# The layout of a routing matrix between SBUF and DRAM, and the place of two reads in one DMA queue

## The reference, cut to what matters

```python
def block(xb):                                   # 128 tokens
    q = (xb @ w_q).reshape(PEER_BLOCK, PEER_HEADS, 2, PEER_DHALF)
    s = jnp.einsum('thpd,hpkd->thpk', q, subkeys)
    s1, i1 = lax.top_k(s[:, :, 0], PEER_TOPK)    # 8 heads, 2 x 128 subkeys, the best 16 of each
    s2, i2 = lax.top_k(s[:, :, 1], PEER_TOPK)
    ...                                          # best 16 of the 256 pair sums: idx, softmax g
    act = gelu(einsum('td,thkd->thk', xb, u[idx]))
    return einsum('thk,thkd->td', g * act, v[idx])
```

## Time and profile before

| | |
|---|---|
| device time, 3 runs | 4415.58, 4419.44 (median), 4424.55 us |
| span of the profiled execution | 4411.2 us |
| PE busy | 4020.6 us (91%) |
| DVE busy | 3174.1 us (72%) |
| ACT busy | 2085.5 us (47%) |
| first layer's experts, down slots | about 1107 to 1686 us of the span |
| second layer's experts, down slots | about 2380 to 2765 us |

### The profile page before, as it was taken

One profiled execution on the slowest core, in us unless ns is written; L12 is line 12 of the kernel. 1 busy time (PEld: TensorE's weight loads), 2 busy tenths in 40 slices (PEclk: granted clock), 3 DMA queues, 4 the chain that ended last, 5 costly groups with the idle time before them and its releaser, 6 DMA issues. The chain is left out here.

```text
span 4411.2 us, 68760 instructions
## 1 busy us (share of the span) xinstructions
PE 4020.6 (91%) x24324; PEld 3590.5 (81%) x24324; DVE 3174.1 (72%) x7302; ACT 2085.5 (47%) x4105; POOL 557.2 (13%) x433
## 2 busy tenths in 40 slices
PE   8979999999999998889999999699887999988898
PEld 5669999999777776689998777598876989887687
DVE  7778999997777776679866677564676656548665
ACT  4434433775333333345675555344455444435453
POOL 0000034223222220005770000000000000000000
PEclk9989999999999999999999999899998999999899
DMA  6245588889999993768898888344435444434353
GB/s 240 96 143 185 177 310 296 287 303 355 332 319 314 325 317 138 232 191 214 221 242 260 262 253 255 131 185 129 139 102 178 185 157 185 157 119 126 131 195 133
DMA packets 417963, 939.83 MB, mean 213 GB/s; under 512 B 53258, under 2 KB 242938, under 8 KB 402058
## 3 DMA queue, kind: packets, MB, share of 16 engines
q1 hardware_dynamic: 362380, 801.86, 54.7%
q0 software_dynamic: 55296, 134.31, 9.8%
HBM read 842.60 MB, written 93.42 MB: 212 GB/s over the span
## 5 line engine op out<-in xcount | busy, mean ns | idle before, releaser
L173 DVE TENSOR_TENSOR w_low__2<-w_raw__2,w_high__2 128x512 fp32r<-128x512 f32 x544 | 361.8, 687 | 123.2 <-ACT w_high__2 L168 111.6
L161 PE MATMUL hidden<-hT_high__2,w_high 128*128 128x384 f32 (+1 forms) x1280 | 423.8, 331 | 11.7 <-DVE w_low L173 11.1
L168 ACT ACTIVATE w_high<-w_raw 128x512 fp32r<-128x512 f32 x576 | 341.5, 625 | 180.7 <-PE side L163 80.4
L173 DVE TENSOR_TENSOR w_low<-w_raw,w_high 128x512 fp32r<-128x512 f32 x576 | 381.3, 685 | 62.3 <-ACT w_high L168 62.2
L162 PE MATMUL hidden<-hT_low__2,w_high 128*128 128x384 f32 (+1 forms) x1280 | 419.4, 328 | 0.0
L163 PE MATMUL hidden<-hT_high__2,w_low 128*128 128x384 f32 (+1 forms) x1280 | 419.2, 328 | 0.0
L168 ACT ACTIVATE w_high__2<-w_raw__2 128x512 fp32r<-128x512 f32 x544 | 321.8, 623 | 85.0 <-DMA w_raw__2<-in_peer_v 30.7
L161 PE MATMUL hidden__3<-hT_high__4,w_high__2 128*128 128x256 f32 x1152 | 326.9, 284 | 0.1
L163 PE MATMUL hidden__3<-hT_high__4,w_low__2 128*128 128x256 f32 x1152 | 323.3, 281 | 0.0
L162 PE MATMUL hidden__3<-hT_low__4,w_high__2 128*128 128x256 f32 x1152 | 323.2, 281 | 0.0
L161 PEld LDWEIGHTS hidden<-hT_high__2,w_high 128*128 128x128 f32 x1280 | 242.8, 190 | 13.5 <-issue 9.4
(11 more groups left out here) (975 smaller groups left out, 12142.2 us busy)
## 6 DMA issues: line engine op xcount, KB each, us to landing
w_raw<-in_peer_u SPq DMA_DIRECT2D x128, 512.0 KB, 5.5
w_raw<-in_peer_v SPq DMA_DIRECT2D x128, 512.0 KB, 5.4
w_raw__2<-in_peer_u SPq DMA_DIRECT2D x128, 512.0 KB, 4.3
w_raw__2<-in_peer_v SPq DMA_DIRECT2D x128, 512.0 KB, 5.0
activated_dram<-activated SPq DMA_DIRECT2D x128, 192.0 KB, 6.4
routing_dram<-routing SPq DMA_DIRECT2D x24, 1024.0 KB, 9.6
routing_chunk<-routing_dram SPq DMA_DIRECT2D x16, 1536.0 KB, 13.9
activated_again<-activated_dram SPq DMA_DIRECT2D x128, 192.0 KB, 5.6
```

The source lines that it names most:

```text
L161: nc.tensor.matmul(out, lhs[0], rhs[0], start=start, stop=False, skip_group_check=True)
L168: return nc.scalar.activation(high, src, ACT.Copy)
L173: return nc.vector.tensor_tensor(low, src, high.bitcast(F32), ALU.subtract)
```

## The change

Two things are changed in `experts`, and the DRAM tensor that goes with them.

The DRAM tensor `routing_dram` was [chunk, partition, (j, t)]: a chunk of 16 tokens was one 8 KB run per partition, written whole, and the read of a group of eight j took, per partition, 24 runs of 512 bytes (8 in the second layer), 1 MiB apart. It becomes [group of eight j, partition, chunk, (8 j, 16 t)]: the read of a group is one run per partition (12 KB, in the second layer 4 KB), and the write of a chunk is 16 runs of 512 bytes per partition.

In SP's slot, the load of the activation (was line 1279) now stands ahead of the reads of the routing group and of the cells.

```diff
                 for k in range(NC):
                     if chunk_last[k] + 3 == s:
                         sp.wait_ge(staged_in, 4 * (k + 1))
-                        sp.dma_start(routed_dram[k], staged[:, k % SR].rearrange("p j t -> p (j t)")) \
+                        sp.dma_start(routed_dram[:, :, k, :].rearrange("b p n -> p b n"),
+                                     staged[:, k % SR].rearrange("p (b j) t -> p b (j t)", j=JC)) \
                             .then_inc(G_stored[k % SR], 16)
+                d = s - UP + AD
+                if 0 <= d < DOWN:
+                    if d >= AD:
+                        sp.wait_ge(weighed_ready, d - AD + 1)
+                    sp.wait_ge(act_stored[d % AR], 16 * (d // AR + 1))
+                    sp.dma_start(act_in[:, d % AD, :], spilled[d]).then_inc(act_loaded[d % AD], 16)
                 if s == read_from:
...
-                        sp.dma_start(G[:, k % 2], routed_dram[:, :, k * JC * GT:(k + 1) * JC * GT]
-                                     .rearrange("c p n -> p c n")).then_inc(G_loaded[k % 2], 16)
+                        sp.dma_start(G[:, k % 2].rearrange("p c j t -> p (c j t)"),
+                                     routed_dram[k].rearrange("p c n -> p (c n)")).then_inc(G_loaded[k % 2], 16)
...
-                d = s - UP + AD
-                if 0 <= d < DOWN:
-                    if d >= AD:
-                        sp.wait_ge(weighed_ready, d - AD + 1)
-                    sp.wait_ge(act_stored[d % AR], 16 * (d // AR + 1))
-                    sp.dma_start(act_in[:, d % AD, :], spilled[d]).then_inc(act_loaded[d % AD], 16)
...
-    routed = [nc.dram_tensor(f"routing_dram_{l}", [n // 16, P, PE_K * 16], F32, kind="Internal").ap()
+    routed = [nc.dram_tensor(f"routing_dram_{l}", [PE_K // 8, P, n // 16, 8 * 16], F32, kind="Internal").ap()
```

## The result

| | before | changed |
|---|---|---|
| device time, median | 4420.76 us (4415.58 to 4424.55, 4 runs) | 4360.32 us (4358.33 to 4368.46, 4 runs) |
| ratio | | 0.9877, 95% interval 0.9852 to 0.9902 |
| span of the profiled execution | 4411.2 us | 4359.6 us |

The change gains 60 us, 1.2%; 54 were forecast (4365 us). A second set of runs of each gave medians of 4424.18 and 4361.27 us.

A forecast was written before the change was run, and what follows sets the result against it. It took late activations behind group reads to stall PE in the down slots, with DVE the bound in the up slots. Terms -45 - 20 - 5 + 15 + 1 = -54 us gave 4365 us; 8-in-10 range 4332 to 4400.

The forecast's parts named there:

- The stalls and their cause: First layer's down slots: the activation behind the group read stalls PE; moving it ahead wins 45 of 51 us.
- The sign I had named for it: First layer's down slots: DVE's wait of `weighed` for the activation would be near zero.
- the grazing of the forecast: First layer's down slots: next activation lands 8.6 us after issue against 8.4 of lead, grazing DVE but not reaching PE.
- The order as the cure: First layer's down slots: the activation issued ahead of the reads no longer waits 8.45 us on SP; 45 us won.
- Rival B: Down slots: the stall only moves one slot back, to the next activation or weights; -20 us, 4399 us; chance 17%.
- Second layer: Second layer's down slots: the activation passes the read and the cells; 20 of 27 us won, bounds 8 and 27.
- Reads at the end of the up slots: First layer's last up slots: one-run reads no longer hold the weight loads; 5 us won, bounds 0 and 7.
- Writes: First layer's up slots: writes of sixteen runs land 1.5 us later, delaying ACT; 15 us lost, bounds 3 and 39.
- rival A: Whole kernel: short-run writes are as good as free and all stalls vanish; -82 us, 4337 us; chance 20%.
- Rival C: Up slots: writes landing in 16.6 us hold the loop; +27 us, 4446 us, deciding from 14.5 us landing; chance 9%.
- The noise: Whole kernel: median of the runs is 8.2 us above the span; about 0.2% (9 us) can be told from no change.

The follow-up runs named there:

- the order alone: Kernel before with only the activation's load moved ahead of the group reads, layout unchanged (long-run writes, short-run reads): 4382.8 and 4378.6 us.
- layout alone: Changed kernel with the activation's load put back behind the group reads, new layout kept: 4378.9 us.
- short both: Changed kernel with a third layout, writes and group reads both in runs of 512 bytes, new order kept: 4382.4 us.
- early writes: Changed kernel with each routing chunk's write issued one slot earlier on SP: 4343.6 and 4347.6 us.
- cells in long runs: Changed kernel with writes one slot earlier, second layer's cells read as one 4 KB run per partition (result not the reference's): 4339.6 us.

## Why the prediction was right, point by point

*The stalls and their cause: right.* Without a hold and with the activation in front, the first layer's 128 down slots take 531 and 534 us, with 533 forecast. I had given 45 us to this; it is 47 between the first profiles and 34 between the second. The step held, but its base was one profile, 5 us above the mean of two. The sign I had named for it did not come: DVE's wait for the activation there is 25.1 and 22.2 us, not near zero. It is the grazing of the forecast, a little more of it than I thought, and ACT's wait for the weights (27.9 us) is its other half; PE has enough in store for nearly all of both.

*The order as the cure: only half right.* The prediction put the whole gain of the first layer under the activation's place in the queue, and worked out the lateness of the next weights and activation by bytes: 8.6 us against 8.4 of lead. That sum is right only with the one-run reads. With the short runs, the order alone leaves 5.2 us of hold for the next weights and 550 to 554 us. Rival B, the stall that moves one slot back, is what the order alone does, and the layout is what keeps it from happening. The prediction does not say that the layout is what takes the hold away. The sum came out right since both edits were in the change; in this it was lucky.

*Second layer: right in kind, base too small.* I took 385.5 us for its down slots, from a row that reads x505; that row ends at 2765 us, and the layer has 512 such matmuls and 390.4 us. So 32 us could be won, not 27. 363.6 us remain, the 365 that were forecast; the gain is 27 us (24 in the second profiles) where I took 20. DVE's wait for activations is 40.5 us, not below 20 as I had said, but PE is idle for only 3.4 us of the stage, so most of it is covered.

*Reads at the end of the up slots: wrong in place.* The hold moved to the loads behind the last two writes, which are now short:

```profile
1067.88 7.81 SPq L1250 DMA_DIRECT2D w_raw<-in_peer_u  x1
...
1077.03 8.04 SPq L1250 DMA_DIRECT2D w_raw<-in_peer_u  x1
```

against 8.36 and 8.47 us behind the reads. PE is idle for 5.8 us of the last 30 us ahead of the down slots before, and for 6.4 us now. That was the lower bound of this term, 0, and it is nearer than the 5 us that I took.

*Writes: the term was 15 us, with 5 off for the reads; the stage as a whole lost 11.8 and 3.3 us.* A mean of 7.5 where the sum had 10. ACT's wait rose from 40 to 50.7 and 46.6 us, not to 60. The changed kernel's trace does not give the landing of these writes, but four others with the same shape do: medians of 11.6 us (layout alone), 10.2 (short both), 9.9 (early writes) and 9.7 (cells in long runs), against 9.6 and 9.2 for long runs. I had taken 1.5 us more; it is 0 to 2. The rule behind rival A, the Trainium skill's line rate from 512 bytes on ("DMA: Bandwidth & Descriptors", section "Specifications"), would have made the cost nothing. With the writes issued early it is nothing, so for these writes the rule errs less than the rows suggested: what cost was the deadline. For the reads it does not hold here: 24 runs of 512 bytes land in 13.9 us, one run of 12 KB in 10.3. Rival C, writes that hold the up slots, had the right loop and a landing too long: single writes take 13.6 us and more, but the 14.5 from which it decides is far from any median. (The DMA share of 0.87 that speaks for it is seven eighths, not three quarters.)

*The noise.* Span to median was taken as 8.2 us. In the changed kernel it is 0.7 us, and between two profiles of before 14 us lie in the spans. So the sum is better set against the stages that the change touches: they lost 62 us between the first profiles and 55 between the second, where it had 54. In the first pair the untouched stages gave 10 us back, and the spans differ by 51.6 us. By the means of the profiles the first layer gave 40 us where the sum had 45, the second 26 where it had 20, and the up slots cost 8 where it had 10: errors that partly cancel, which is luck.

## What to carry to other kernels

In this kernel a DMA in many short runs cost its queue more than its bytes did: look at the instruction behind it on SP, and at who waits for what that one brings. Moving the urgent load in front passed the hold to the next load and won about half of what the stalls cost in the first layer; making the runs long removed it. When short runs must go somewhere, put them on the side whose completion has slack, and buy that slack by issuing them as soon as their data are there: one slot earlier was worth 13 to 18 us, about a quarter of the whole change.

## What the runs showed of the hardware that I had not expected

How long SP is held goes with the short runs still queued. Behind a read of 3072 runs of 512 bytes in the first layer's down slots, SP's next DMA took 6.0 to 8.8 us when it was issued 0.6 us later, and 2.9 to 6.1 when it came about 3.2 us later. 2048 runs (the second layer's two reads) held it 2.6 to 4.9 us at once. 1024 (the cells alone, in the changed kernel) did not hold the next weights, issued 1.5 us after:

```profile
2440.26 0.43 SPq L1279 DMA_DIRECT2D routing_cells_read<-scattered_dram  x1
2441.73 0.33 SPq L1250 DMA_DIRECT2D w_raw__2<-in_peer_v  x1
```

Writes hold too: the last two of 2048 such runs held the loads 2.7 and 0.5 us behind them for about 8 us. The other 22 held theirs, 4.6 us behind or more, for 1.6 us at most (2.4 in the second profile). But the count is not all of it: at the end of the up slots of before, a read of 3072 runs still held a load 4.5 us behind it for 8.36 us. What else lengthens it there no run shows; the DMA engines moved 416 GB/s from 1068 to 1076 us, more than the 307 of the down slots.

And the DMA engines move 334 GB/s on average over 531 us of down slots, at a busy share of 0.92, with PE idle for 1.9 us in all, where 307 GB/s and 0.90 went with 32.7 us of idle: the share said nothing of the stall.
